# Order of the first norm in a two-block transformer kernel: high and low parts of all eight chunks of x first, squares and sums behind them

## The reference, cut to what matters

```python
def rms_norm(x, w):
    x32 = x.astype(f32)
    y = x32 * lax.rsqrt(jnp.mean(x32 * x32, axis=-1, keepdims=True) + EPS)
    return (y * w.astype(f32)).astype(x.dtype)

h = rms_norm(x, norm1_w[l])
cols = split_cols(h @ w_in[l], IN_SIZES)      # columns for four mixers
```

## Time and profile before

| | us |
|---|---|
| median of three runs | 1797.21 |
| the profiled execution, its own time | 1797.75 |
| its span in the profile | 1796.0 |
| TensorE busy in the span | 1772.6 |
| GpSimd busy | 1094.7 |
| VectorE busy | 746.4 |
| ScalarE busy | 496.9 |

### The profile page before, as it was taken

One profiled execution on the slowest core, in us unless ns is written; L12 is line 12 of the kernel. 1 busy time (PEld: TensorE's weight loads), 2 busy tenths in 40 slices (PEclk: granted clock), 3 DMA queues, 4 the chain that ended last, 5 costly groups with the idle time before them and its releaser, 6 DMA issues.

```text
span 1796.0 us, 22448 instructions
## 1 busy us (share of the span) xinstructions
PE 1772.6 (99%) x8530; PEld 1423.6 (79%) x8530; DVE 746.4 (42%) x1267; ACT 496.9 (28%) x955; POOL 1094.7 (61%) x1149
## 2 busy tenths in 40 slices
PE   8999999999999999999999999999999999999998
PEld 5676767888888887778888888777888888888886
DVE  6338655330023236243005373555433587215532
ACT  3226662220022111312004232555300222222232
POOL 5543406777777787666776675545678574445442
PEclk9999999999999999999999999999999999999999
DMA  4720012232223223222322222221223222322231
GB/s 177 238 85 27 25 48 82 95 102 97 94 95 100 99 95 117 71 83 87 103 94 71 82 71 86 71 71 65 78 96 105 82 94 95 105 94 94 96 104 59
DMA packets 47055, 163.06 MB, mean 91 GB/s; under 512 B 5539, under 2 KB 6755, under 8 KB 46564
## 3 DMA queue, kind: packets, MB, share of 16 engines
q1 hardware_dynamic: 43200, 154.75, 25.6%
q10 hardware_dynamic: 3748, 6.87, 1.3%
HBM read 158.56 MB, written 2.12 MB: 89 GB/s over the span
## 4 chain that ended last, share of the span: by engine, by line
PE 92%; DVE 3%; ACT 2%; issue 1%; ACTq 1%; DMA 1%; SPq 0%; DVEq 0%
PE bank L811 90%; DVE sq_sum L1864 1%; PE bank L1156 1%; PE bank L1202 1%; DMA x_sb<-in_x 0%; ACT sq L1412 0%; DVE tmp L1869 0%; ACTq L1561 0%; ACTq L1555 0%; ACT sb_e L1769 0%; DVE h_lo L1926 0%; DVE cmp_xt L2121 0%; DVE sq_parts L1896 0%; ACT rstd_t L1470 0%; ACT att_pt L1711 0%
## 5 line engine op out<-in xcount | busy, mean ns | idle before, releaser
L2515 POOL TENSOR_TENSOR w_lo_t<-w_raw,w_hi_t 128x256 fp32r<-128x256 f32 (+1 forms) x892 | 822.4, 950 | 168.0 <-ACT w_hi_t L1496 149.6
L2510 POOL TENSOR_SCALAR w_hi_t<-w_raw 128x1024 fp32r<-128x1024 f32 (+1 forms) x221 | 239.8, 1085 | 476.9 <-PE bank L811 430.9
L811 PE MATMUL bank<-h_hi,w_hi_t 128*128 128x512 f32 x1044 | 419.6, 402 | 8.6 <-ACT h_hi L1533 8.6
L811 PE MATMUL bank<-h_hi,w_lo_t 128*128 128x512 f32 x1044 | 407.6, 391 | 0.0
L811 PE MATMUL bank<-h_lo,w_hi_t 128*128 128x512 f32 x1044 | 401.4, 389 | 0.0
L811 PEld LDWEIGHTS bank<-h_hi,w_hi_t 128*128 128x128 f32 x1044 | 197.1, 189 | 60.7 <-issue 18.8
L811 PEld LDWEIGHTS bank<-h_hi,w_lo_t 128*128 128x128 f32 x1044 | 197.3, 189 | 41.1 <-issue 1.4
L811 PEld LDWEIGHTS bank<-h_lo,w_hi_t 128*128 128x128 f32 x1044 | 195.8, 188 | 42.2 <-issue 1.7
L811 PE MATMUL bank<-hid_hi,w_hi_t 128*128 128x512 f32 x432 | 168.0, 389 | 0.0
L811 PE MATMUL bank<-hid_lo,w_hi_t 128*128 128x512 f32 x432 | 168.0, 389 | 0.0
L811 PE MATMUL bank<-hid_hi,w_lo_t 128*128 128x512 f32 x432 | 168.0, 389 | 0.0
(11 more groups left out here) (360 smaller groups left out, 2490.5 us busy)
## 6 DMA issues: line engine op xcount, KB each, us to landing
w_raw<-in_w SPq DMA_DIRECT2D x276, 512.0 KB, 3.2
y<-in_w SPq DMA_DIRECT2D x6, 512.0 KB, 5.5
x_sb<-in_x SPq DMA_DIRECT2D x4, 512.0 KB, 7.8
x_sb<-in_x ACTq DMA_DIRECT2D x2, 1024.0 KB, 5.2
out_y<-x_sb SPq DMA_DIRECT2D x8, 256.0 KB, 2.4
u_raw<-in_w SPq DMA_DIRECT2D x2, 512.0 KB, 5.4
toep<-table ACTq DMA_DIRECT2D x4, 256.0 KB
decay<-in_decay SPq DMA_DIRECT2D x1, 1024.0 KB, 4.7
```

Source lines behind the costliest of these rows:

```text
L811: return pe.matmul(out, lhs, rhs, start=start, stop=stop, **kw)
L2510: pool.tensor_scalar(hi[:, 0:cols], raw[:, 0:cols], 1.0, 0.0, ALU.mult, ALU.add).then_inc(*did("w_hi", i))
L2515: ins = pool.tensor_tensor(lo[:, piece], raw[:, piece], hi.bitcast(F32)[:, piece], ALU.subtract)
```

## The change

The loop that interleaves the steps u and sq is replaced by all eight u, followed by all eight sq. `sqs("n1", KD)` gives `("sq", "n1", 0)` to `("sq", "n1", 7)`; it would add a step `sq_parts` for the norms in `IN_PARTS`, and "n1" is not one of them.

```diff
-    for c in range(KD + 3):
-        run([("u", "n1", c)] * (c < KD) + [("sq", "n1", c - 3)] * (c >= 3))
+    run([("u", "n1", c) for c in range(KD)] + sqs("n1", KD))
```

## The result

22 executions of the changed kernel took 1801.72 us in the median (1796.30 to 1805.99), 22 of the kernel before 1797.27 us (1794.26 to 1800.30). The ratio is 1.0023, 95% interval 1.0015 to 1.0031: slower by 4.2 us in the mean (4.45 us between the medians), against 3.2 us forecast. The profiled execution of the changed kernel is one of the fastest, 1796.73 us with a span of 1794.9 us, and it is faster than the profiled one of before (1797.75). Part of that is TensorE's clock: behind the first rise of the clock, near 16 us, this one has no *low stretch* (a stretch at the lower of the clock's two levels) up to its end, the one of before has one of 7 us. So the two profiles are compared place by place, and the times over many executions.

The account below looks back on a forecast made before the run. TensorE, busy 1772.6 of 1796.0 us, was taken to bound the kernel. A 3.2 us wait for the late sums, other terms 0, gave 1797.21 + 3.2 = 1800.4 us, 0.18% slower; 8-in-10 range 1797.5 to 1802.2 us.

Parts of the forecast that it names:

- likeliest case alone: Whole kernel: TensorE waits 2.7 to 3.55 us at full clock, giving 1799.6 to 1801.2 us; chance 0.66.
- the central sum: Whole kernel: median 1797.21 us plus a 3.2 us wait of TensorE gives 1800.4 us.
- TensorE can only start the norm later, and the slack is small: First norm on TensorE: its start at 24.25 us is fixed by TensorE's own order; sum 6 is ready 0.61 us earlier.
- High parts, low parts and the two DMAs cost and bring nothing: ScalarE's high parts, VectorE's low parts, DMAs onehot and rb_t: moved earlier by the change, gain 0 and cost 0.
- The sums' chain: VectorE's low parts and sums before the first norm: held by GpSimd's instructions, they make TensorE wait 3.2 us.
- The two cases: Sum 4 against GpSimd's high part: GpSimd first, TensorE waits 3.55 us; sum 4 first, 2.7 us.
- the two sides meet within 0.04 us: VectorE against GpSimd: sum 4 may start at 21.90 us, GpSimd's high part starts at 21.86 us.
- The delay is paid once, in full: Chain from r_h to sq_parts of cq: the first norm's delay arrives there too, the 2.6 us wait staying unchanged.
- The clock: Rival, TensorE in the new gap: clock falls, +1 to +2.5 us on top, 1801.4 to 1803.3 us; chance 0.14.

Follow-up runs that it names:

- e1: The changed kernel run again with no edit; median 1804.12 us, ratio 1.0037 to the kernel before.
- e11: The kernel before with the squares four chunks behind the high parts instead of three; median 1799.20 us, ratio 1.0020.
- e4: The kernel before with the squares five chunks behind the high parts instead of three; median 1800.11 us, ratio 1.0020.
- e9: The kernel before with one extra matmul ahead of each bias table and six ahead of sq_parts of cq; median 1795.92 us, ratio 0.9998.
- e8: The kernel before with ten extra matmuls in the gap ahead of sq_parts of cq; median 1796.44 us, ratio 0.9996.
- e6: The changed kernel with GpSimd's slot of nq1 (high and low part) put behind sum 6; median 1797.38 us, ratio 1.0005.
- e5: The changed kernel with ten extra matmuls on TensorE ahead of its wait for sum 6; median 1801.38 us, ratio 1.0024.
- e12: The changed kernel with ten extra matmuls ahead of TensorE's wait for sum 6, run for more executions; median 1802.03 us, ratio 1.0027.
- e7: The kernel before with GpSimd's low parts in four pieces from nq0 on and norm n1 in front of nq0; median 1797.50 us, ratio 1.0007.
- e3: The changed kernel with norm n1 behind six of nq0's eight chunks instead of two; median 1800.16 us, ratio 1.0023.
- e10: The kernel before with one more TensorE wait ahead of norm n1's sum, for the low part of nq1's slot; median 1799.86 us, ratio 1.0017.
- e2: The changed kernel with GpSimd's low parts cut into four pieces from nq0 on instead of from cqr on; median 1798.06 us, ratio 1.0007.

## Why the prediction was right, and where it was off

The forecast was 1800.4 us, the result 1801.72: inside the range, but above the likeliest case alone (1799.6 to 1801.2). By the recorded chances the result had 0.61 to lie within 0.2% of before and 0.36 to be slower by more; it is slower by 0.23%. The waits came out somewhat shorter than forecast (2.8 us of base), and the clock, which the central sum had at nothing, filled the rest and more. That the sum lands within 1.3 us is partly luck: e1's seven executions of the same kernel lie at 1804.12 us, outside the range.

- **TensorE can only start the norm later, and the slack is small.** Right in direction: e11 and e4 cost 1.3 and 1.6 us for one and two steps of lag. The 0.61 us is that of one execution; in e9's profile sum 6 is done 1.7 us ahead of the norm (22.83 and 24.54), in e8's 0.4 us.
- **High parts, low parts and the two DMAs cost and bring nothing.** Right as far as e6 shows: it has all of them moved and the median of before, though a base 1.3 us higher. Low 5 and low 6 were held as forecast (1.52 and 2.86 us in the profile after), and the DMAs left at 12.09 us.
- **The sums' chain.** Sum 1 was forecast to start at 18.85 and did at 19.10; sum 2 at 20.34, it did at 20.54, behind 0.76 us of idleness for which I had 0.81. The two cases were forecast at waits of 2.7 and 3.55 us; TensorE waits 2.02 us in the one profile (it came to the norm 0.66 us later there) and 3.32 us in the other. Over 22 executions the base rises by 2.8 +- 0.2 us, where I had taken 3.2. That the two sides meet within 0.04 us was not the point: GpSimd's slot starts anywhere over 2 us (above), and in the four profiles of the changed order with the slots as they were (after, e1, e5, e12) sums 4 to 6 met it each time.
- **"The delay is paid once, in full", through the chain to cq.** Half right, and by another path. In e1 the gap at cq stayed at 2.4 us; in the profile after it shrank by 1.1 us. This is the chain that ended last, between the norm and the queue of ScalarE that feeds cq (before, after, e7):

```profile
26.89 0.64 ACT r_h L1473
...
27.55 0.04 DVE kv_raw L1971
...
27.09 25.80 PE bank L810 x110
...
52.91 0.70 ACT rstd_t L1469
...
23.64 27.16 PE bank L811 x116
...
50.83 0.70 ACT rstd_t L1470
```

  Before, the chain leaves TensorE at r_h and runs over VectorE and the DMAs, as the prediction has it. But TensorE's own path was level with it there: the later norm's matmuls end near 49.96 us, and ScalarE's rstd_t starts at 50.00. After, in e1 and in e7 it stays on TensorE's own matmuls, up to those of that later norm, and ScalarE waits for them. It starts at 48.94 us before, at 51.86 us after and at 49.77 us in e7. So the changed kernel's delay arrives there in full (2.92 us) through TensorE's own list; and the earlier r_h of e7 brought nothing, since the later norm came 0.83 us later than before. What follows is ScalarE's queue, which needs 3.0 to 4.4 us in the 14 profiles to issue two DMAs of 16 rows (`y<-y`). It took 4.13 us before and 3.01 us after, and this is the 1.1 us by which the gap at cq shrank. The profile after, in the chain that ended last:

```profile
57.98 2.36 ACTq L1560
...
60.38 0.61 ACTq L1560
```

- **The clock.** This is the term that I mis-sized. It was a rival with a chance of 0.14 and a price of 1 to 2.5 us; in fact the low time goes from 4.7 to 8.5 us in the 22 executions (9.7 in all 29), so that it costs 1.9 to 2.5 us in the mean, nearly as much as the waits. (The rival's own sum is a little off: 1800.4 + 2.5 is 1802.9 us, not 1803.3.) Its mechanism shows in e3: the clock fell inside the gap of 3.86 us and the norm's four matmuls took 1.9 us longer, where the rival had 1.7. I had read the earlier trace rows as if a gap of 2.6 us were harmless since one of that length was. e1's gap of 2.4 us at cq was followed by the lower clock at 70.1 us, and the one of before was not. The Trainium skill (TensorE: Matmul & The Clock Gate, Why this matters for your kernels) warns of idle gaps between matmul bursts beyond a length that e1's first gap, 3.3 us, reaches and its second, 2.4 us, does not; both were followed by the lower clock, and the measurement decides. That a gap caused it is shown by neither. The low time rises with the late norm (e10 makes it rise with 1.8 us of gap and nothing else changed, in e6 it does not rise), but filling the gap does not clearly undo it (e5, e12).

What stays open is how a late norm makes the clock fall more often when TensorE has no gap. The six profiles of e2, e4, e5, e10, e11 and e12 have a low stretch that begins between 34.0 and 36.5 us, behind the bias tables; e3, whose tables come later, has one at 38.5 us, besides the one from 28.3 to 35.5 us that began in its gap; those of before, e6, e7, e8 and e9, with the norm in time or nearly so, have none there, but neither have the two of the changed kernel. A run that moves the tables alone would tell, and was not made. Nor does a profile say, for an execution that it did not record, where its low time lay.

## What to carry to other kernels

Where two engines take turns at something, a delay of half a microsecond does not cost half a microsecond: look at what the other engine will have started by then, and count the whole of its instruction. Before work is regrouped so that one engine does all of one kind first, see what the interleaving hid: here a low part covered the square that the next sum needed, and GpSimd's slot met only the last sum. And when a stage already waits, judge a few microseconds over twenty executions with their clocks, since one profile of either kernel can show the slower one as faster.

## What the runs showed of the hardware

- VectorE and GpSimd hold each other for whole instructions when both read SBUF: 2.86 us for a low part that takes 0.74 alone and 2.67 us for a sum that takes 0.68. Beside GpSimd's low parts cut in four, a low part or a sum of VectorE took about 1.22 us, so that it was held for half a microsecond, but nearly every one was (the low parts from 10.07 us took 7.42 us for six, against 8.82). The evacuations from PSUM behind the norm were not held: 0.68 us at 27.55 us under GpSimd's low part, and 0.68 or 0.69 us each in e2 and e7. The Trainium skill (SBUF — State Buffer, Who interferes with whom) says as much: an instruction of VectorE with two SBUF inputs contends with GpSimd's reads, one with at most one SBUF input does not, unless it runs in a mode that takes both ports.
- Which of the two goes first is decided finely: 22.01 against about 22.07 us in e1. At 8.3 us VectorE's second low part and GpSimd's high part change places between executions (1.41 us for two low parts in e1, 2.24 in e2).
- TensorE's clock fell in a stretch where it was busy throughout, behind narrow matmuls (e12, above), not only behind idle gaps.
- The first rise of TensorE's clock differs between executions: the first matmul of 0.39 us instead of 0.63 stands at 11.4 us in e3 and e11, at 15.5 us in e1 and behind 16 us in the profile after. GpSimd's slot behind TensorE's first banks moves with it by up to 2 us.
